# An expert lookup taken tile by tile: V rows gathered per token and summed in four column groups, one ring of 14 slots

## The reference, cut to what matters

```python
q = einsum('nd,dhc->nhc', hf, w_peer_q)                      # 8 heads x 256
s1, s2 = q[..., :128] @ k1.T, q[..., 128:] @ k2.T            # 128 keys each
v1, i1 = top_k(s1, 16); v2, i2 = top_k(s2, 16)
cand = v1[..., :, None] + v2[..., None, :]                   # 256 pairs
sc, sel = top_k(cand, 16)                                    # 16 of them per head
idx = take(i1 * 128 + i2, sel)                               # 8 x 16 = 128 experts per token
gate = softmax(sc)
a = gelu(einsum('cd,ckd->ck', hc, peer_u[idx]))              # 128 dot products of 1024 per token
out = einsum('ck,ckd->cd', gate * a, peer_v[idx])            # weighted sum of 128 rows per token
```

## Time and profile before

| what | value |
|---|---|
| median of three runs | 2582.07 us |
| span of the profiled execution | 2587.8 us |
| busy: PE, DVE, ACT, POOL | 82%, 49%, 20%, 50% of the span |
| moved by DMA | 657.67 MB, 254 GB/s over the span |
| gathers | 544 of U, 544 of V |

### The profile page before, as it was taken

How to read it: one execution, slowest core, us unless ns; L and a number is a source line. 1 busy time by engine, 2 the same in 40 slices (tenths; PEclk the granted TensorE clock), 3 DMA queues, 4 the chain that set the end, 5 groups by cost and what they waited for, 6 DMA issues and landing times.

```text
span 2587.8 us, 26580 instructions
## 1 busy us (share of the span) xinstructions
PE 2109.7 (82%) x7116; PEld 1111.9 (43%) x7116; DVE 1259.6 (49%) x2894; ACT 504.9 (20%) x1274; POOL 1301.4 (50%) x1228
## 2 busy tenths in 40 slices
PE   7999997997999999888888787676676666776767
PEld 5864443576888646334334333222222222222223
DVE  2114332252101145675576567567567557557653
ACT  2223222452000012121121211212112112111112
POOL 0003221000000016677777777777777777777775
PEclk9999998988999999899999999999999999999999
DMA  6213222105222028899999999999999999999998
GB/s 199 66 49 103 82 83 93 66 1 173 73 73 74 19 68 320 300 375 371 374 369 378 379 345 381 379 348 354 360 358 339 363 335 343 371 360 343 392 374 335
DMA packets 264701, 657.67 MB, mean 254 GB/s; under 512 B 27479, under 2 KB 116504, under 8 KB 264607
## 3 DMA queue, kind: packets, MB, share of 16 engines
q0 software_dynamic: 160768, 572.60, 59.1%
q1 hardware_dynamic: 103847, 83.97, 10.9%
HBM read 652.48 MB, written 4.18 MB: 254 GB/s over the span
## 4 chain that ended last, share of the span: by engine, by line
PE 42%; DMA 23%; issue 15%; POOL 10%; DVE 6%; ACT 1%; DVEq 1%; POOLq 1%; SPq 0%; ACTq 0%
PE bank L555 23%; DMA arena<-in_peer_v_dram,arena 19%; POOL arena L511 10%; PE bank L1024 10%; DMA arena<-in_peer_u_dram,arena 3%; PE bank L551 3%; PE bank L716 2%; PE bank L736 2%; DVE arena L1674 2%; DVEq L1621 1%; PE bank L717 1%; PE bank L878 1%; PE bank L802 1%; PE bank L822 0%; ACT arena L1054 0%
## 5 line engine op out<-in xcount | busy, mean ns | idle before, releaser
L1024 PE MATMUL bank<-arena 128*128 128x512 f32 x2176 | 1072.3, 623 | 391.8 <-DMA arena<-in_peer_v_dram,arena 351.3
L511 POOL DMA_INDIRECT arena<-in_peer_u_dram,arena x544 | 621.3, 1142 | 765.9 <-DVE arena L1661 581.4
L1674 DVE CUSTOM_DVE_ANT_0 arena<-arena 128x1024 f32<-128x1024 f32 x544 | 651.2, 1224 | 475.6 <-DMA arena<-in_peer_u_dram,arena 470.0
L1024 PEld LDWEIGHTS bank<-arena 128*128 128x128 f32 x2176 | 385.2, 193 | 1064.1 <-issue 909.6
L555 PE MATMUL bank<-arena 128*128 128x272 f32 (+8 forms) x2844 | 684.0, 399 | 29.5 <-DMA arena<-in_w_x_out_dram 11.1
L511 POOL DMA_INDIRECT arena<-in_peer_v_dram,arena x544 | 609.5, 1120 | 169.7 <-issue 130.4
L555 PEld LDWEIGHTS bank<-arena 128*128 128x128 f32 (+1 forms) x2844 | 513.7, 190 | 188.7 <-issue 75.3
L1054 ACT ACTIVATE arena<-bank 128x512 f32<-128x512 f32 (+16 forms) x315 | 139.9, 465 | 752.6 <-PE bank L555 428.4
L505 POOL DMA_DIRECT2D arena<-in_cache_k_rope_dram x128 | 69.0, 539 | 332.3 <-issue 332.3
L1305 ACT ACTIVATE arena<-arena 128x128 f32<-128x128 f32 x544 | 162.6, 387 | 14.0 <-DVE arena L1682 14.0
L551 PE MATMUL bank<-arena 128*128 128x128 f32 (+5 forms) x1048 | 130.8, 263 | 41.0 <-DVE arena L1405 10.5
(11 more groups left out here) (138 smaller groups left out, 1009.7 us busy)
## 6 DMA issues: line engine op xcount, KB each, us to landing
arena<-in_cache_kv_latent_dram SPq DMA_DIRECT2D x128, 128.0 KB, 2.0
arena<-in_w_in_dram SPq DMA_DIRECT2D x24, 512.0 KB, 5.9
arena<-in_w_peer_q_dram SPq DMA_DIRECT2D x20, 512.0 KB, 10.4
arena<-in_peer_u_dram,arena POOLq DMA_INDIRECT x544, 6.3
arena<-in_peer_v_dram,arena POOLq DMA_INDIRECT x544, 6.3
arena<-in_w_in_dram SPq DMA_DIRECT2D x6, 1024.0 KB, 6.7
arena<-in_cache_mem_k_dram SPq DMA_DIRECT2D x8, 512.0 KB, 4.2
arena<-in_cache_mem_v_dram SPq DMA_DIRECT2D x8, 512.0 KB, 5.6
```

The lines of the kernel that those rows point to most:

```text
L511: pool.indirect_dma_start(out=ring[:, k % RING], out_offset=None, in_=table[0], in_offset=IndirectOffsetOnAxis(ap=ix, axis=0)).then_inc(la ...
L1024: last = pe.matmul(bank[:, 2 * b + c], diag[:, k], vring[:, k % RING, c * 512:(c + 1) * 512], start=(k == 0), stop=(k == 15))
L1674: dve.tensor_tensor_reduce(uring[:, k % RING], uring[:, k % RING], h[:], 1.0, 0.0, ALU.mult, ALU.add, act_a[:, k:k + 1]).then_inc(u_free, 1)
```

## The change

- **Order.** The lookup goes tile by tile: first the 128 U gathers of tile 0, then the V gathers of each tile in turn with the U gathers of the next (`gather_order`). The sample tokens' 32 U and 32 V end it. Nothing is looped; every engine's program is written out.
- **V per token.** The tile's expert numbers are transposed (`turn_ids`, `ids_out`), so that a V gather fetches the 128 experts of one token: partition = expert. U gathers stay as they were.
- **Weights.** The 128 x 128 weights are transposed by PE once per tile (`turn_weights`), and ACT spreads them into `zw`, for each token a block of 32 columns in which one column holds its weights and the others are zero (`spread`). The diagonals go.
- **Sums.** Four V tiles make a quad. Token 32j + i belongs to quad i and to column group j: a 128x32 matmul adds into partitions 32j to 32j + 31. Slots are freed per quad.
- **Ring.** U and V share one ring of 14 slots, filled in the written order. From the ninth slot on POOL waits until all residuals are added.
- **Start and queries.** Tile 0 gets all 16 of its query sums first, four at a time between the residual products, the other 416 columns behind; 32 loads into three buffers instead of 20 into two. The first scores stand behind the third residual product.
- **DVE.** A pick is one piece, before 32 products. The copy of the scores and the hand-over copies go; one add of a sum per tile, and the finals of a tile two tiles later.

```diff
+def gather_order():
+
+    out = [("u", 0, k) for k in range(P)]
+    for p in range(TILES - 1):
+        for n in range(P):
+            out.append(("v", p, n))
+            if p < TILES - 2 or n < NS:
+                out.append(("u", p + 1, n))
+    return out + [("v", TILES - 1, n) for n in range(NS)]
+
+
+ORDER = gather_order()
+PLACE = {entry: s for s, entry in enumerate(ORDER)}
...
-        uring = at(61, [RING, D])
-        vring = at(127, [RING, D])
-        hA, hB = at(6, [D]), at(14, [D])
-        diag = at(159, [16, P])
-        sc = at(54.5, [4, NKEY])
+        ring = [at(61 + 4 * i, [D]) for i in range(8)] + [at(133 + 4 * i, [D]) for i in range(RING - 8)]
+        zw = at(93, [P, NS])
...
-            for i, j in enumerate(Q_LOADS):
-                if i >= 2:
-                    sp.wait_ge(pq_mm, i - 1)
-                sp.dma_start(wpq[:, i % 2], wq[:, :, j]).then_inc(ld_pq[i % 2], 16)
-            sp.wait_ge(w_done, 2 * ITS - 1)
+            for i in range(2 * QJ):
+                if i >= 3:
+                    sp.wait_ge(pq_mm, i - 2)
+                sp.dma_start(wpq[i % 3], wq[:, :, i % QJ]).then_inc(ld_pq[i % 3], 16)
...
-            def gather(ring, land, k, table, ix):
-                pool.sem_inc(carrier, 1)
-                pool.indirect_dma_start(out=ring[:, k % RING], out_offset=None, in_=table[0],
-                                        in_offset=IndirectOffsetOnAxis(ap=ix, axis=0)).then_inc(land[k % RING], 16)
-
-            pool.wait_ge(id_next, 1)
-            for k in range(16):
-                pool.wait_ge(u_free, k + 1)
-                gather(uring, u_in, k, peer_u, idN[:, k:k + 1])
...
+            def gather(s, table, ix):
+                pool.indirect_dma_start(out=ring[s % RING], out_offset=None, in_=table[0],
+                                        in_offset=IndirectOffsetOnAxis(ap=ix, axis=0)).then_inc(land[s % RING], 16)
+
+            for s, (kind, p, n) in enumerate(ORDER):
+                if s == 8:
+
+                    pool.wait_ge(wo_ev, 2 * TILES)
+                    pool.memset(zw[:], 0.0).then_inc(z_zero, 1)
+                if s >= RING:
+                    was, pp, pn = ORDER[s - RING]
+                    if was == "u":
+                        pool.wait_ge(u_free, u_count(pp, pn))
+                    else:
+                        pool.wait_ge(v_free, v_quads(pp, pn))
+                if kind == "u":
+                    if n % 32 == 0:
+                        pool.wait_ge(id_next, 4 * p + n // 32 + 1)
+                    gather(s, peer_u, idU[:, p % 2, n:n + 1])
+                else:
+                    if n == 0:
+                        pool.wait_ge(idt_ev, p + 1)
+                    t = (n % 4) * (32 if p < TILES - 1 else 8) + n // 4
+                    gather(s, peer_v, idT[:, p % 2, t:t + 1])
...
+            first_queries(0)
+            resid(2)
+            first_scores(0)
+            turn_h(1)
+            first_queries(1)
+            resid(3)
+            first_scores(1)
+            turn_h(2)
+            first_queries(2)
+            resid(4)
+            first_scores(2)
+            turn_h(3)
+            turn_h(4)
+            first_queries(3)
+            first_scores(3)
...
-            def weigh(it, b, j=None):
-
-                pe.wait_ge(acc_free, it * 2 + (b + 1))
-                for k in range(16):
-                    if j is not None and k == 7:
-                        queries(j)
-                    if j is not None and k == 12:
-                        key_scores(j)
-                    pe.wait_ge(diag_done, it * 32 + (16 * b + k + 1))
-                    pe.wait_ge(v_in[k % RING], it * 64 + 16 * (2 * b + k // RING + 1))
-                    for c in range(2):
-                        last = pe.matmul(bank[:, 2 * b + c], diag[:, k], vring[:, k % RING, c * 512:(c + 1) * 512],
-                                         start=(k == 0), stop=(k == 15))
-                    last.then_inc(v_free, 1)
...
+            def weigh(p):
+
+                pe.wait_ge(z_done, p + 1)
+                if p >= 2:
+                    pe.wait_ge(acc_free, p - 1)
+                quads = QUADS if p < TILES - 1 else NS // 4
+                for i in range(quads):
+                    at_slot = [PLACE["v", p, 4 * i + j] for j in range(4)]
+                    for s in at_slot:
+                        pe.wait_ge(land[s % RING], land0[s % RING] + 16 * (s // RING + 1))
+                    for c in range(2):
+                        for j in range(4):
+                            last = pe.matmul(bank[32 * j:32 * j + 32, 2 * (p % 2) + c], zw[:, 32 * j + i],
+                                             ring[at_slot[j] % RING][:, c * 512:(c + 1) * 512],
+                                             start=(i == 0), stop=(i == quads - 1))
+                    last.then_inc(v_free, 1)
+                    if p < TILES - 2 and i == 20:
+                        turn_ids(p + 1)
+
+            turn_ids(0)
+            pe.wait_ge(wo_ev, 2 * TILES)
+            for p in range(TILES):
+                if p < TILES - 1:
+                    turn_weights(p)
+                weigh(p)
...
-            def diagonals(it, b, last_step=False):
-                act.wait_ge(w_done, it * 2 + (b + 1))
-                for k in range(16):
-                    act.wait_ge(v_free, it * 32 + (16 * b + k + 1))
-                    act.sem_inc(carrier, 1)
-                    act.activation(diag[:, k], ident[:, 1 if last_step else 0], ACT.Copy,
-                                   scale=wts[:, k:k + 1]).then_inc(diag_done, 1)
...
+            def gelu(p):
+                w = P if p < TILES - 1 else NS
+                act.wait_ge(u_free, u_count(p, w - 1))
+                if p >= 1:
+                    act.wait_ge(w_done, p)
+                act.activation(act_g[:, 0:w], act_a[:, p % 2, 0:w], ACT.Gelu).then_inc(gelu_done, 1)
+
+            def spread(p):
+
+                act.wait_ge(wt_mm, p + 1)
+                if p == 0:
+                    act.wait_ge(z_zero, 1)
                 else:
-                    src = hn[:, DynSlice((it + 1) % 4, 1)].rearrange("p a d -> p (a d)")
-                act.activation(dst, src, ACT.Copy).then_inc(done, 1)
+                    act.wait_ge(v_free, QUADS * p)
+                w = 32 if p < TILES - 1 else 8
+                dst = zw.rearrange("p (j i) c -> p j (i c)", j=4)[:, :, 0:33 * w - 32:33]
+                src = bank[:, 5, 0:P] if p < TILES - 1 else blockT[:]
+                copy(dst, src.rearrange("p (j i) -> p j i", j=4)).then_inc(z_done, 1)
...
+            def products(p, k0, k1):
+
                 for k in range(k0, k1):
-                    dve.wait_ge(u_in[k % RING], land0 + U0 + 16 * (k // RING + 1))
-                    dve.tensor_tensor_reduce(uring[:, k % RING], uring[:, k % RING], h[:], 1.0, 0.0, ALU.mult, ALU.add,
-                                             act_a[:, k:k + 1]).then_inc(u_free, 1)
-
-            def weights(n, diags, gates):
-
-                dve.wait_ge(gelu_done, n)
-                if diags is not None:
-                    dve.wait_ge(diag_done, diags)
-                tt(wts[:], act_g[:], gates, ALU.mult).then_inc(w_done, 1)
-
-            def add_sum(it, b):
-                dve.wait_ge(v_free, it * 32 + 16 * (b + 2))
-                dve.wait_ge(acc_free, it * 2 + (b + 2))
-                if isinstance(it, int):
-                    y = hall[:, it % 4 if it < ITS - 1 else slot(0)]
+                    s = PLACE["u", p, k]
+                    dve.wait_ge(land[s % RING], land0[s % RING] + 16 * (s // RING + 1))
+                    dve.tensor_tensor_reduce(ring[s % RING], ring[s % RING], hn[:, p], 1.0, 0.0, ALU.mult, ALU.add,
+                                             act_a[:, p % 2, k:k + 1]).then_inc(u_free, 1)
...
-            def one_step(it):
-                first = isinstance(it, int) and it == 0
-                if first:
-                    products(it * 64 + 32, hB, h_b, it + 1, 0, PICK_ROW)
-
-                dve.wait_ge(w_done, it * 2 + 1)
-                dve.wait_ge(sc_ev, (it + 1) // 4 * 4 + 5)
-                dve.wait_ge(g_b, it + 1)
-                pick_sides(it + 1)
-                if not first:
-                    products(it * 64 + 32, hB, h_b, it + 1, 0, PICK_ROW)
-                pick_pairs(it + 2)
-                products(it * 64 + 32, hB, h_b, it + 1, PICK_ROW, 16)
-                weights(it * 2 + 2, it * 32 + 16, gB[:])
-                add_sum(it, 0)
-                dve.wait_ge(w_done, it * 2 + 2)
-                hand_over()
-                products(it * 64 + 64, hA, h_a, it + 2)
-                weights(it * 2 + 3, it * 32 + 32, gN[:, 0:16])
-                add_sum(it, 1)
-                dve.wait_ge(id_a, it + 2)
-                dve.tensor_copy(idB[:], idA[:, 16:32]).then_inc(id_b, 1)
...
+            for p in range(TILES - 1):
+                for q in range(4):
+                    pick(4 * p + q + 1)
+                    if p == 0 and q == 3:
```

(54 more changed lines are left out.)

407 lines of the change are left out of this document (189 added, 218 removed).

## The result

The changed kernel took 2717.55 us (median; 2714.48 to 2724.72), the kernel before beside it 2584.32 us: a ratio of 1.054, 95% interval 1.051 to 1.057. The direction was forecast (slower, 0.74), the size was not: 2633 us were forecast, 85 us or 3.1% too few. The time lies inside the range, near its upper end. That is luck: this end stood for slow quads, which did not come.

A forecast was written before the change was run, and what follows sets the result against it. It took DMA transfers to bound the lookup, 1.28 us per gather, with losses where DVE holds up POOL. Phase 0 to 1238, quarters 1145 to 2383, then 239 and tail 15.8: span 2639, less 5.7 = 2633 us; range 2565 to 2725.

The forecast's parts named there:

- Start: Queries and residuals up to the first product: ids at 969 us, 9 us later than before; products begin at 1023.
- Phase 0: The 128 U of tile 0 alone, bound by DVE: 236 us, ending at 1238 with 133 gathers issued.
- The 12 quarters: Phases 1 to 3, each quarter a whole pick, 32 products and 64 gathers: 12 x 95.2 + 3 = 1145 us, to 2383.
- the stop: POOL waits per quarter for a free slot while DVE does the whole pick: 9.8 us.
- the burst: Back-to-back products behind a pick slow POOL's gathers to 2.29 us each: 3.5 us lost per quarter.
- 64 gathers at 1.28 = 81.9: Transfer floor of a quarter, each gather at the 1.28 us that 410 GB/s gives.
- Rest: After phase 3: 187 gathers without a pick at 1.28, 239 us, then a tail of 15.8 us; span 2639.
- Quads: Matmuls per four V tokens on PE: 2.9 us each, costing nothing up to 3.6 us, so 0 in the sum.
- POOL gets its pace back: Rival: without the semaphore increment gathers keep 1.24 us beside products; 2553 us, chance 0.18 with milder forms.
- Quads serial: Rival: quads run one after another or at the lower clock, 6.9 us each; 2857 us, chance 0.14 with milder forms.
- Half of that: Rival: only half of POOL's pace back, quarters of 91 to 92 us; 2589 us, within 0.5%, chance 0.08.

The follow-up runs named there:

- run 1: The changed kernel with the pick in two halves behind tile 0, 16 products between the halves: 2632.53 us, 1.021 of before.
- run 9: The kernel before with its pick in one piece in steps 6 to 14, its 10 products behind the pick: 2661.01 us, 1.027 of before.
- run 3: The changed kernel with picks 8 to 16 left out, gathers and products as many as before: 2613.19 us, 1.014 of before.
- run 2: The changed kernel with the norm rows in PSUM from tile 1 on, pick still whole: 2623.76 us, 1.018 of before.
- run 7: The changed kernel with the pick in halves and the norm rows in PSUM together, 14 slots: 2524.25 us, 0.975 of before.
- run 8: The changed kernel with the pick in halves, the norm rows in PSUM and a ring of 16 slots: 2507.89 us, 0.969 of before.
- run 6: The changed kernel with five unneeded matmuls behind each quad to keep TensorE busy: 2749.52 us, 1.062 of before.
- run 4: The changed kernel with V in token order, so a quad's four matmuls go to one column group, one after another: 2967.74 us, 1.151 of before.
- run 12: The kernel before with both copies of the norm rows (hA and hB) in PSUM: 2502.23 us, 0.971 of before.

## Why the prediction was right or wrong

Its span was 2639, the measured one is 2714.4: 75 us too few. Three parts make them up, in its own steps.

- **Start: nearly right.** Ids came at 967.6 (forecast 969), the first product at 1015.4 (1023).
- **Phase 0: 10 us late.** It ended at 1248.1, forecast 1238. That is 18 us more for its products and picks, less the 8 of the earlier start. DVE waited 16.8 us for U rows (22 waits) where the sum had 4. U gathers meet products here all the time; I had priced that only until DVE had caught up.
- **The 12 quarters: 56 us, the step that failed.** They took 2449.4 - 1248.1 = 1201.3 us, forecast 1145. The step was "12 x 95.2", and of its terms:
  - the stop, 9.8: measured 114.0 / 12 = 9.5. Right, and shown from both sides, by runs 1 and 9.
  - the burst, 3.5: three gathers of 1.98 and one of 1.68, right.
  - **64 gathers at 1.28 = 81.9: wrong.** I took 1.28 from a 5 us window at 410 GB/s and let it hold beside products everywhere. That products lengthen gathers outside the bursts too, I had put at nothing. Beside them a gather takes 1.38 us (1.39 in run 3). For the some 50 gathers of a quarter outside the burst and the pick that is about 5.2 us: 81.9 + 9.5 + 3.5 + 5.2 = 100.1.

  1.28 is not impossible beside such products. The window of the earlier trace rows has two of them (2529.90 and 2532.45), and the last step of the kernel before held this pace for 20 us and more:

```profile
2520.00:2540.00 20.00, 15.19 (x33) 5.32 (x32) 9.53 (x16) 0.00 (x0) 15.13 (x17) 1.00 1.03 410
```

  There a gather begins some 0.2 us before each product's end (2530.92 against 2531.13) and takes 1.02 us. With one operand in PSUM the moment no longer matters (runs 2, 7, 8). So the fault was to take a stretch where the two engines happened to miss each other for the rule.

  POOL's busy time over whole quarters or steps gives the sum without a pace assumed (windows of the changed kernel, of the kernel before, and of run 2):

```profile
1257.81:2361.03 1103.22, 314.12 (x1413) 61.12 (x1413) 631.61 (x1473) 17.08 (x29) 776.10 (x704) 0.58 0.90 337
1584.73:2430.45 845.72, 583.26 (x1153) 201.47 (x1152) 537.20 (x1260) 132.15 (x351) 655.58 (x577) 0.97 0.96 357
1255.48:2276.20 1020.72, 313.92 (x1417) 61.29 (x1421) 629.76 (x1473) 18.75 (x31) 659.75 (x704) 0.59 0.92 363
```

  64 gathers keep POOL busy for 70.6, 72.7 and 60.0 us. At 0.94 us each it would be 60, so products lengthen the gathers of a quarter by 10.6 us, those of an old step by 12.7, and those of run 2 by nothing. The old step's loss of 11.7 us was thus mostly this. I had explained part of it by two bursts, some 7 us, and left the rest without a cause; the change met it too.
- **Rest: 9 us.** From the end of phase 3 to the end were 265.0 us, forecast 2639 - 2383 = 256. The tail behind the last gather is 2714.4 - 2693.8 = 20.6 us, not 15.8. I took 6.3 us from issue to landing; with DVE silent and the DMA share at 1.03 the gathers from 2668 on took this long (us min/median/max):

```profile
DMA to landing us min/median/max: 10.0/10.6/11.1
```

  The other 4 us are the 187 gathers, which took 244.4 us instead of 240; some 30 of them still meet products.
- **Quads: right that they set no pace, too short in size.** They take 3.3 to 3.6 us at the low clock (2.9 forecast, limit 3.6), and POOL's waits for them are 20.7 us in all where the sum had 0. The margin was thinner than "costs nothing": 5.6 us of waits with 16 slots, 179.4 with 12. The 2.38x for three column tiles in the Trainium skill ("TensorE: Matmul & The Clock Gate", section on packing small matmuls), which led me to 2.9, is passed by these four: at a granted clock of 1.00 a quad in run 6 takes 1.92 us where 16 records of 0.43 would take 6.9.
- **The rivals.** *POOL gets its pace back*: it did not. The 0.30 us between gathers are there without the increment, and gathers of 1.98 us too. It named the right place, products against gathers, with the wrong cause. *Quads serial*: they are not, and run 4 shows the price, 2968. *Half of that*: excluded by 100.3.

The changed kernel thus lost to the one before by the pick in one piece (7.1 us per quarter by run 1, 6.5 per step by run 9) and by 48 gathers not issued in phase 0 (some 55 to 61 us by count, not by an experiment), and hardly by its new matmuls. The loss beside products is common to both.

## A version that beats both

The new order with the pick in halves, norm rows in PSUM and 16 slots (run 8: 2507.89 us, 0.969 [0.966, 0.973]), and the old order with only the norm rows moved to PSUM (run 12: 2502.23 us, 0.971 [0.968, 0.974]) are equal within the measurement. Run 12 is far the smaller edit. Both may have more to give, which was not tried: in run 12 the second to sixth steps still take 89 to 94 us, since the banks are not free yet, where the later ones take 84.8, and run 8 still has its phase 0.

## What to carry to other kernels

Before you forecast a change, close the sum of the loss that the profile shows: if a step of 93.6 us has 11.7 us above its floor and your causes explain 7, the rest has a cause that the change may meet too. Take a stage's pace from the middle of the stage and from many operations, not from its best 5 us. If an engine's operations with two SBUF operands run beside gathers that POOL issues, try one operand in PSUM first: here an edit of a few lines was worth 3%.

## What the runs showed that I had not expected

- A gather takes 0.94 us beside nine back-to-back products with one operand in PSUM, and 1.98 us beside products with both in SBUF; the products take 1.22 us either way.
- A gather that is under way when such a product begins keeps 0.94 us; one that begins inside it ends 0.81 us behind it. So the same products and gathers run at 1.28 us or at 1.39 us per gather, by how they happen to fall.
- Four column groups side by side: 16 records in 1.92 us at a granted clock of 1.00 and in 3.3 to 3.6 us at 0.57 (between the levels of 1.2 and 2.4 GHz), with PE idle for 7 to 9 us ahead of each quad; into one group 8.9 us at 0.83 (mean from 1250 to 2450).
- Ring depth is not linear: 12, 14 and 16 slots gave 2884, 2718 and 2670 us.
